# A mixture-of-experts loop on TensorE whose items hold 96 tokens in place of 128

## The reference

```
hn = rms_norm(h, attn_norm[l]);  p = hn @ w_in[l]
h  = h + merged(retention, rwkv7, latent attention) @ w_o[l]
hn = rms_norm(h, ffn_norm[l])
layer 0: h = h + (silu(hn @ wg) * (hn @ wu)) @ wd          # 1024 -> 2816 -> 1024
layer 1: logits = hn @ router; top 2 of 8 experts, softmax over the two
         for e in range(8): out += comb[:, e] * (silu(hn @ wg[e]) * (hn @ wu[e])) @ wd[e]   # 1024 -> 3584 -> 1024
final rms_norm
```

## Time and profile before

| | |
|---|---|
| median of 3 runs | 1890.06 us |
| the profiled execution | 1890.98 us, its span 1888.9 us |
| PE (TensorE matmul) busy | 1853.0 us, 98% |
| PEld (TensorE weight load) busy | 1506.2 us, 80% |
| DVE (VectorE) busy | 1442.5 us, 76% |
| ACT (ScalarE) busy | 1167.1 us, 62% |
| chain that ended last | PE 87%; line L1852 alone 47% |
| mean granted TensorE clock | 0.995 |

### The profile page before, as it was taken

The page is one execution under the profiler, slowest core; times in us unless marked ns, Lnnn a source line. Parts: engine busy times, 40 slices in busy tenths (PEclk is TensorE's granted clock), DMA queues, the critical chain, the costliest instruction groups (busy, mean ns, idle before and its releaser), DMA issues.

```text
span 1888.9 us, 26671 instructions
## 1 busy us (share of the span) xinstructions
PE 1853.0 (98%) x10298; PEld 1506.2 (80%) x10298; DVE 1442.5 (76%) x1487; ACT 1167.1 (62%) x1153; POOL 173.7 (9%) x164
## 2 busy tenths in 40 slices
PE   8999999999999999999999999999999999999998
PEld 7878766788888787767888888888888888888886
DVE  4778575644556785755988989888889899898997
ACT  4575324543444753345777777777777777777776
POOL 1263003100002630040000000000000000000000
PEclk9999999999999999999999999999999999999999
DMA  9642223654566422225999999999999999999995
GB/s 315 207 158 101 90 90 134 217 193 147 188 220 199 158 101 90 90 90 194 358 371 341 368 343 355 366 339 370 342 358 371 352 355 362 342 368 341 360 370 216
DMA packets 182541, 487.79 MB, mean 258 GB/s; under 512 B 5896, under 2 KB 12676, under 8 KB 173640
## 3 DMA queue, kind: packets, MB, share of 16 engines
q1 hardware_dynamic: 177296, 477.50, 69.1%
q0 software_dynamic: 1488, 5.57, 0.9%
q10 hardware_dynamic: 3688, 3.74, 0.7%
HBM read 482.03 MB, written 1.05 MB: 256 GB/s over the span
## 4 chain that ended last, share of the span: by engine, by line
PE 87%; DVE 7%; DMA 3%; ACT 2%; issue 1%; POOL 0%; ACTq 0%; SPq 0%; DVEq 0%
PE bank L1852 47%; PE bank L1249 25%; PE bank L1462 2%; PE bank L1801 2%; PE bank L1433 1%; PE bank L1863 1%; PE bank L1241 1%; DMA ring<-w_o_dram 1%; PE bank L1821 1%; DVE y_rwkv L1920 1%; DVE ring_lo L1920 1%; DMA cst<-const_dram 1%; DVE tmp L1920 1%; DMA ring<-moe_w_down_dram 1%; DMA h<-x_dram 0%
## 5 line engine op out<-in xcount | busy, mean ns | idle before, releaser
L1920 DVE TENSOR_TENSOR w_lo<-ring,w_hi 128x2048 fp32r<-128x2048 f32 x337 | 767.2, 2289 | 112.5 <-ACT w_hi L1151 104.5
L1151 ACT ACTIVATE w_hi<-ring 128x2048 fp32r<-128x2048 f32 x320 | 612.4, 1917 | 122.6 <-PE bank L1852 110.2
L1852 PE MATMUL bank<-w_hi,xg_hi 128*128 128x512 f32 x896 | 354.8, 396 | 1.1 <-DVE w_lo L1920 1.1
L1852 PE MATMUL bank<-w_hi,xg_lo 128*128 128x512 f32 x896 | 349.3, 390 | 0.0
L1852 PE MATMUL bank<-w_lo,xg_hi 128*128 128x512 f32 x896 | 349.0, 389 | 0.0
L1852 PEld LDWEIGHTS bank<-w_hi,xg_hi 128*128 128x128 f32 x896 | 168.8, 188 | 37.5 <-DVE w_lo L1920 4.2
L1852 PEld LDWEIGHTS bank<-w_hi,xg_lo 128*128 128x128 f32 x896 | 168.2, 188 | 35.9
L1852 PEld LDWEIGHTS bank<-w_lo,xg_hi 128*128 128x128 f32 x896 | 168.4, 188 | 33.5 <-issue 0.2
L1852 PE MATMUL bank<-w_hi,ehT_hi 128*128 128x512 f32 x448 | 176.9, 395 | 0.1
L1852 PE MATMUL bank<-w_hi,ehT_lo 128*128 128x512 f32 x448 | 174.7, 390 | 0.0
L1852 PE MATMUL bank<-w_lo,ehT_hi 128*128 128x512 f32 x448 | 174.4, 389 | 0.0
(11 more groups left out here) (434 smaller groups left out, 3027.0 us busy)
## 6 DMA issues: line engine op xcount, KB each, us to landing
ring<-moe_w_gate_dram SPq DMA_DIRECT2D x57, 2048.0 KB, 7.5
ring<-moe_w_up_dram SPq DMA_DIRECT2D x56, 2048.0 KB, 7.7
ring<-moe_w_down_dram SPq DMA_DIRECT2D x56, 2048.0 KB, 9.5
ring<-w_in_dram SPq DMA_DIRECT2D x26, 2048.0 KB, 8.0
ring<-w_branch_dram SPq DMA_DIRECT2D x6, 2048.0 KB, 8.3
ring<-ffn_w_gate_dram SPq DMA_DIRECT2D x5, 2048.0 KB, 7.9
ring<-ffn_w_up_dram SPq DMA_DIRECT2D x5, 2048.0 KB, 7.9
ring<-ffn_w_down_dram SPq DMA_DIRECT2D x5, 2048.0 KB, 8.5
```

The source lines that it names most:

```text
L1151: A.activation(w_hi[:, q % PARTS, :], ring[:, i, o:o + HALF], ACT.Copy).then_inc(s.hi_ready, 1)
L1852: ins = M(dst, a, w, start=start and n == 0, stop=stop and n == 2, skip_group_check=True)
L1920: return V.tensor_tensor(out_, a, b, op)
```

## The change

The constant `CAP = 96` takes the place of `P = 128` wherever it meant "tokens of an item". An item's token columns 0 to 95 are computed; the tiles that rest in the array keep their distance of 128 elements (512 bytes) in SBUF and are read as `[:, x, 0:CAP]`. An expert now needs a second item over 96 tokens and a third over 192: `GROUPS = 3` tables of slots and weights in place of 2, up to `MORE = 5` items beyond the 8 in place of 3, and a longer computation of the list `items`. The moved columns of gate, up, down and scatter stay 512, and the list of matmuls is the same.

```diff
+CAP = 96
+GROUPS = -(-SEQ // CAP)
+MORE = (SEQ * 2 - NE) // CAP
-    c["slots"] = np.tile(np.arange(P, dtype=np.float64), (P, 1))
+    c["slots"] = np.tile(np.where(i < CAP, i, 0.5), (P, 1))
+    c["later"] = np.tile(2 * NE - np.arange(2 * NE, dtype=np.float64), (P, 1))
...
# gather and its two readers
-  ins = M(b[:, i * P:(i + 1) * P], hn[:, t, n * P:n * P + P], sel[:, t, :], start=t == 0,
+  ins = M(b[:, i * CAP:(i + 1) * CAP], hn[:, t, n * P:n * P + P], sel[:, t, 0:CAP], start=t == 0,
-  ins = A.activation(xg_hi[:, 4 * u + i, :], b[:, i * P:(i + 1) * P], ACT.Copy,
+  ins = A.activation(xg_hi[:, 4 * u + i, 0:CAP], b[:, i * CAP:(i + 1) * CAP], ACT.Copy,
-  ins = V.scalar_tensor_tensor(out=xg_lo[:, c, :], in0=b[:, i * P:(i + 1) * P],
+  ins = V.scalar_tensor_tensor(out=xg_lo[:, c, 0:CAP], in0=b[:, i * CAP:(i + 1) * CAP],
...
# gate, up, down
-  ins = three(b[:], xg_hi[:, x, :], xg_lo[:, x, :], q % PARTS,
+  ins = three(b[0:CAP, :], xg_hi[:, x, 0:CAP], xg_lo[:, x, 0:CAP], q % PARTS,
-  ins = three(b[:], ehT_hi[:, x, :], ehT_lo[:, x, :], q % PARTS,
+  ins = three(b[0:CAP, :], ehT_hi[:, x, 0:CAP], ehT_lo[:, x, 0:CAP], q % PARTS,
...
# turn, scatter, transposes of sel
-  ins = TR(b[:, c * P:(c + 1) * P], ehm[:, j % 2, c:512:4], ident)
+  ins = TR(b[:, c * CAP:(c + 1) * CAP], ehm[0:CAP, j % 2, c:512:4], ident[0:CAP, 0:CAP])
-  ins = M(b[:], selT[:, t * P:(t + 1) * P], part[:, 512 * u:512 * u + 512], start=i == 0,
+  ins = M(b[:], selT[0:CAP, t * P:(t + 1) * P], part[0:CAP, 512 * u:512 * u + 512], start=i == 0,
-  ins = TR(b[:, t * P:(t + 1) * P], sel[:, t, :], ident)
+  ins = TR(b[0:CAP, t * P:(t + 1) * P], sel[:, t, 0:CAP], ident)
...
# SiLU, product, and the halves of ehT on ScalarE and VectorE
-  A.activation(esg[:, j % 2, :], item_product(f"eg{j}")[:], ACT.Silu).then_inc(s.freed_act, 1)
+  A.activation(esg[0:CAP, j % 2, :], item_product(f"eg{j}")[0:CAP, :], ACT.Silu).then_inc(s.freed_act, 1)
-  A.activation(ehT_hi[:, 4 * j:4 * j + 4, :],
-               item_product(f"eT{j}")[:].rearrange("p (c n) -> p c n", c=4),
+  A.activation(ehT_hi[:, 4 * j:4 * j + 4, 0:CAP],
+               item_product(f"eT{j}")[:, 0:4 * CAP].rearrange("p (c n) -> p c n", c=4),
-  tt(ehm[:, j % 2, :], b[:], esg[:, j % 2, :], ALU.mult).then_inc(s.freed_vec, 1)
+  tt(ehm[0:CAP, j % 2, :], b[0:CAP, :], esg[0:CAP, j % 2, :], ALU.mult).then_inc(s.freed_vec, 1)
...
# routing: slots per group, flags over 96 and over 192 tokens
-  for i in range(2):
-      step(V.tensor_scalar(spos[:, i, :, :], R(5), -1.0 - P * i, None, ALU.add))
+  for i in range(GROUPS):
+      step(V.tensor_scalar(spos[:, i, :, :], R(5), -1.0 - CAP * i, None, ALU.add))
-  free(V.tensor_scalar(f[:, 0:8], b[0:1, 16:24], P + 0.5, None, ALU.is_gt), "rank.1")
+  step(V.tensor_scalar(f[:, 0:8], b[0:1, 16:24], CAP + 0.5, None, ALU.is_gt))
+  free(V.tensor_scalar(f[:, 8:16], b[0:1, 16:24], 2 * CAP + 0.5, None, ALU.is_gt), "rank.1")
# list of items: 12 small operations with 6 waits between them become 14 with 8 waits
-  step(V.tensor_copy(items[0:1, 0:25], f[:, 32:57]), s.items_ready)
+  step(V.tensor_copy(items[0:1, 0:27], f[:, 56:83]), s.items_ready)
```

More of the change, by code:

```diff
@@ L412, in build @@
     rope_tmp = sb("rope_tmp", [P, 1024], where=B + 49152)
+    pos_f = sb("pos_f", [P, T], where=B + 51200)
     ix_hi = sb("ix_hi", [P, KD, SEQ], F32R, where=ec_at - 4096)
@@ L686, in _ @@
         sp.wait_ge(s.items_ready, 1)
-        n_items = sp.value_load(items[0:1, 24:25], min_val=SURE, max_val=SURE + 3)
+        n_items = sp.value_load(items[0:1, 26:27], min_val=SURE, max_val=SURE + MORE)
         with sp.If(n_items > SURE):
             with sp.Fori(SURE, n_items) as item:
-                e = sp.value_load(items[0:1, bass.ds(item + 12, 1)], min_val=0, max_val=NE - 1)
+                e = sp.value_load(items[0:1, bass.ds(item + NE + MORE, 1)], min_val=0, max_val=NE - 1)
                 expert_panels(e, item)
@@ L1134, in _ @@
         act.wait_ge(s.items_ready, 1)
-        n_items = act.value_load(items[0:1, 24:25], min_val=SURE, max_val=SURE + 3)
+        n_items = act.value_load(items[0:1, 26:27], min_val=SURE, max_val=SURE + MORE)
         with act.Fori(0, n_items) as item:
@@ L1811, in _ @@
         pe.wait_ge(s.items_ready, 1)
-        n_items = pe.value_load(items[0:1, 24:25], min_val=SURE, max_val=SURE + 3)
+        n_items = pe.value_load(items[0:1, 26:27], min_val=SURE, max_val=SURE + MORE)
         def scatter(item, b_of):
@@ L2464, in _ @@
         settle()
-        step(V.tensor_scalar(selT[:], cst[:, 0:SEQ], 0.0, None, ALU.mult))
+        step(V.tensor_scalar(selT[0:CAP, :], cst[0:CAP, 0:SEQ], 0.0, None, ALU.mult))
         step(V.memset(weight[:], 0.0))
         select(0)
-        step(V.tensor_scalar(f[:, 8:16], C("experts")[0:1, :], -1.0, 8.0, ALU.mult, ALU.add))
+        more = slice(0, MORE)
+        over, first, upper = f[:, 24:32][:, more], f[:, 32:40][:, more], f[:, 40:48][:, more]
+        step(tt(f[:, 64:80], C("later")[0:1, :], f[:, 0:16], ALU.mult))
@@ L2470, in _ @@
+        step(V.reduce_sum(f[:, 56 + 26:56 + 27], f[:, 0:16], AX.X))
         settle()
-        step(tt(f[:, 8:16], f[:, 8:16], f[:, 0:8], ALU.mult))
-        step(V.reduce_sum(f[:, 56:57], f[:, 0:8], AX.X))
+        step(V.max(f[:, 16:24], f[:, 64:80]))
         settle()
-        step(V.max(f[:, 16:24], f[:, 8:16]))
+        step(V.tensor_scalar(over, f[:, 16:24][:, more], -1.0, 2.0 * NE, ALU.mult, ALU.add))
+        step(V.tensor_scalar(f[:, 82:83], f[:, 82:83], float(NE), None, ALU.add))
         settle()
-        step(V.tensor_scalar(f[:, 40:44], f[:, 16:20], -1.0, 24.0, ALU.mult, ALU.add))
@@ L2477, in _ @@
-        step(V.tensor_copy(f[:, 32:40], C("experts")[0:1, :]))
-        step(V.tensor_copy(f[:, 44:52], C("experts")[0:1, :]))
-        step(V.tensor_scalar(f[:, 52:56], f[:, 16:20], -1.0, 8.0, ALU.mult, ALU.add))
-        step(V.tensor_scalar(f[:, 56:57], f[:, 56:57], float(NE), None, ALU.add))
+        step(V.tensor_scalar(over, over, 2.0 * NE - 1, None, ALU.min))
         settle()
-        step(V.tensor_scalar(f[:, 52:56], f[:, 52:56], float(NE - 1), None, ALU.min))
-        step(V.tensor_scalar(f[:, 40:44], f[:, 40:44], float(2 * NE * T // 2 + NE - 1), None, ALU.min))
+        step(V.tensor_scalar(upper, over, NE - 0.5, float(NE), ALU.is_gt, ALU.mult))
@@ L2484, in _ @@
         settle()
-        step(V.tensor_copy(items[0:1, 0:25], f[:, 32:57]), s.items_ready)
+        step(tt(first, over, upper, ALU.add))
+        step(tt(over, over, upper, ALU.subtract))
+        settle()
+        step(V.tensor_scalar(f[:, 56 + NE:56 + NE + MORE], first, float(NE * T), None, ALU.add))
+        step(V.tensor_copy(f[:, 56 + 2 * NE + MORE:56 + 2 * NE + 2 * MORE], over))
+        step(V.tensor_copy(f[:, 56:56 + NE], C("experts")[0:1, :]))
+        step(V.tensor_copy(f[:, 56 + NE + MORE:56 + 2 * NE + MORE], C("experts")[0:1, :]))
@@ L2529, in _ @@
         gathered_lo(lambda job: ahead(dve, job), 0)
-        n_items = dve.value_load(items[0:1, 24:25], min_val=SURE, max_val=SURE + 3)
+        n_items = dve.value_load(items[0:1, 26:27], min_val=SURE, max_val=SURE + MORE)
         with dve.Fori(0, n_items) as item:
-            next_column = dve.value_load(items[0:1, bass.ds(item + 1, 1)], min_val=0, max_val=NE * T + NE - 1)
+            next_column = dve.value_load(items[0:1, bass.ds(item + 1, 1)], min_val=0, max_val=NE * T * (GROUPS - 1) + NE - 1)
             def item_product(job):
@@ L2571, in _ @@
                     dve.wait_ge(s.x_hi_ready, item * 9 + (j + 3))
-                    tt(ehT_lo[:, 4 * j:4 * j + 4, :], b[:].rearrange("p (c n) -> p c n", c=4),
-                       ehT_hi[:, 4 * j:4 * j + 4, :].bitcast(F32), ALU.subtract).then_inc(s.freed_vec, 1)
+                    tt(ehT_lo[:, 4 * j:4 * j + 4, 0:CAP], b[:, 0:4 * CAP].rearrange("p (c n) -> p c n", c=4),
+                       ehT_hi[:, 4 * j:4 * j + 4, 0:CAP].bitcast(F32), ALU.subtract).then_inc(s.freed_vec, 1)
                 if q == 35:
```

18 lines of the change are left out of this document (9 added, 9 removed).

## The result

The changed kernel takes 1898.33 us (median of 5 runs, 1896.89 to 1901.92) against 1891.79 for the kernel before (median of 5 runs): a ratio of 1.0040, with an interval of 1.0029 to 1.0051. That is 0.4% slower. One of the five runs of the kernel before took 2428.71 us; it is left out of the ratio, and without it that median is 1890.93. The forecast was 1888.4 with a range up to 1893.5, so both the direction and the range were missed. The profiled execution took 1896.89 us.

What follows compares the result with a forecast made beforehand. TensorE was taken as the bound, with the price of its fp32r matmuls the whole question. All terms were 0 except 1.7 us gained at exposed loads: 1890.06 - 1.7 = 1888.4 us, range 1873 to 1893.5.

Steps and rivals of the forecast that it cites:

- the row at the low clock: At clock 0.50, 512-column matmuls take 0.4275 us against 0.4267 streamed; taken as evidence that fewer resting columns gain zero.
- the matmuls of gate, up and down: Expert loop's 4032 matmuls: resting 96 columns in place of 128 gains zero, at most 13.5 us.
- the 13.4 ns: Time each gate, up or down matmul takes beyond its 0.2133 us stream of 512 columns at full clock.
- Gather: Item start, 32 matmuls: moving columns fall to 96, but the 128-column load sets the pace, gain 0; otherwise 6.8 us.
- Turn: Transposes of `ehm`: the strided 128-column load sets the pace, so 96 moving columns gain 0; otherwise 5 us.
- What follows a gather or a turn: Exposed load and shorter stream before it, eight places per item: 0.027 us less each, 1.7 us gained in all.
- ScalarE and VectorE: Copies into `ehT_hi`, `ehT_lo`, `xg_hi`, `xg_lo` lose a quarter of their columns; that goes into idle time: 0.
- Routing: Extra table, flag, weights and longer list before the loop: hidden, 0; without cover 0.65 us once.
- A: Gate, up and down matmuls speed up with fewer resting columns: 0.2234 us each, 1874.9 us total; chance 0.18.
- B: Gather and turn are bound by the moving stream, so they shorten: 1876.6 us, gather alone 1881.6; chance 0.09.
- D: A ninth item is needed once an expert has 97 tokens: 123.8 us more, 2013.9 us; chance 0.01.
- C: Loads under 128 columns are prepared worse: over 300 us, or mildly 1897.3 us through 64 exposed loads; chance 0.12.

Runs made afterwards that it cites:

- the sweep: Kernel before, with gate and up panel pairs resting on different column counts from 128 down to 32, in two kernels: never under the full tile's 226.9 ns per matmul.
- the resting columns alone: Kernel before with only gate, up and down resting on 96 columns, all else at 128: 1900.11 us against 1890.76, ratio 1.0050.
- the rest of the change alone: Changed kernel with gate, up and down resting on 128 columns again: 1891.98 us against 1890.76, ratio 1.0006.

## Why the prediction was wrong, point by point

**The step that failed** is "I take zero, by the row at the low clock, and keep 13.5 us for the range", for the matmuls of gate, up and down. The term is +2.3 ns on the average, +9.3 us over 4032 matmuls, where the text allowed 0 to -13.5. In the steady middle of a panel it is +3.3 ns (226.7 to 230.0); the average is lower because in the kernel before the six matmuls after each turn already took 228 to 236 ns. The sign that the prediction had named for itself showed it: gather to gather 124.71 us in place of 123.6, more than its 0.5 off. Two things were wrong in it. The rows it used speak of whether a load is exposed as a whole, and are read to 10 ns, while the term is 3; and it bounded an unknown cost from one side only, with the reason that less rests. A bound on the slow side was due, because no row of before had an fp32r matmul on 96 resting columns. That the 13.4 ns are no piece of the load that shrinks with its columns was right, and the sweep shows it: 32 columns cost 231.6. But the row at the low clock didn't say that they are a constant, and they aren't: distance and counts move them between 13 and 20 ns.

**What bounds the kernel** was right: TensorE by its stream of fp32r matmuls, and the price of one is "the whole question".

**Gather.** Right at 0: 32 matmuls in 3.71 us in place of 3.74; (3.71 - 0.25) / 31 is 0.112 each, so the load of 128 columns sets the pace. **Turn.** Right at 0 for the transposes.

**What follows a gather or a turn.** Right. From the last full matmul to the second after the turn it was 0.94 us, now it is 0.91; the loads after a gather went from 0.11 to 0.09 apart.

```profile
1327.41 0.39 PE L1852 MATMUL bank<-w_hi,xg_lo 128*128 128x512 f32 x1
...
1328.35 0.39 PE L1852 MATMUL bank<-w_lo,xg_hi 128*128 128x512 f32 x1
```

It takes both halves of the change, as the text had it: with the resting columns alone that stretch is 0.940 us, with the rest of the change alone 0.938, with both 0.914 (before 0.937). In sum it is 1.5 us, by the item of the resting columns alone against that of the full change: (124.90 - 124.71) x 8. The forecast had 1.7.

**ScalarE and VectorE** at 0: right, they wait more than before. **Routing** at 0: right. Behind the cast of the longer list VectorE still idles before `xg_lo`, 0.29 us where the earlier trace rows had 1.07:

```profile
880.10 0.17 DVE L2496 CAST items<-it_f 1x27 int32<-1x27 f32 x1
...
882.01 0.99 DVE L2520 SCALAR_TENSOR_TENSOR xg_lo<-bank,gains,xg_hi 128x96 fp32r<-128x96 f32 x4 [0.29 <-ACT xg_hi L1127]
```

So 0.78 us of that cover are used, where I had estimated 0.5 to 0.65; some 0.15 us of it is ScalarE, whose copies of 96 columns are ready that much sooner after the gather's start (`xg_lo` starts 3.09 us after it in place of 3.24).

**The rivals.** A (pace follows the resting columns, 1874.9) was wrong in sign. At 512 moving columns no panel of any kernel ran steadily below 226.7. B was wrong, by the gather. D was wrong: x896 again. C had the sign and, in its mild form, nearly the time (1897.3), but its mechanism is refuted: the loads became shorter and the 64 exposed places faster; the loss sits where the load is hidden. That the two numbers agree is chance.

On the fast load that rival C weighed: the Trainium skill (TensorE: Matmul & The Clock Gate, "Weight-path perf modes — Fast Weight Load (FWL) and DoubleRow") says that fewer than 128 resting columns forfeit it. Here the load of 96 columns lasts 0.161 to 0.163 us and that of 128 lasted 0.188; it shrank with the columns, so nothing fast was lost. That would agree with the rule's exclusion of FP32 if fp32r falls under it, which the page doesn't say. The Trainium skill (the same page, "Back-to-back issue gap") gives about 216 ns for an isolated matmul of 512 columns and about 131 ns for one in a sustained stream of loads and matmuls; the fp32r matmuls of such a stream took 226.7 to 233.3 here depending on the placement, above both, and for this kernel the measurement decides.

**What was right in the end.** With the tiles placed at 144 bytes the steady pace is the 226.7 that I forecast, and the kernel takes 1888.17 us, where the forecast said 1888.4. That the two agree to 0.2 us is in part chance: the item is 0.38 us shorter than before (123.44 against 123.82), 3.0 us in eight, where the forecast had 1.7, and the medians differ by 2.5. The forecast described that kernel, not this one. The change as made kept the distance that suits 128 columns.

## What to carry to other kernels

When TensorE is busy all the time, read the distance between starts over nine or more matmuls, not the busy share or the duration of one: both stayed as they were while every matmul became 1.4% dearer. The pace of this stream of fp32r matmuls depended on the distance in the partition between the resting and the moving tile together with both column counts, so a change of any of the three (a narrower item, a tile moved to make room) needs that pace measured anew, over a few distances in steps of 16 bytes. Look at it panel by panel and item by item, because a mean can hide two paces, and prefer a distance at which all panels are fast. And bound an operation that no row shows from both sides, also when it has less to do.

## What the runs showed of the hardware that was not expected

- Moving the resting tiles by 128 bytes, with only addresses changed, costs 1.2% (1912.14 against 1891.01 us); moving resting and moving tiles together costs nothing (1890.55 against 1890.78). For full tiles the effect repeats with 256 bytes (226.9 at 0 and at 256).
- The spacing runs in short patterns, not in noise: 229, 229, 231, 231 ns in the changed kernel, 226 and 227 in the kernel before, 229 and 237 at 128 bytes. All steady values lie between 226.7 and some 233.5 ns for 512 moving columns, 13 to 20 ns over the bare stream of 213.3.
- 32 resting columns (231.6) are dearer than 128 (226.9) at distance 0.
- At some distances the same panel has two steady paces: 226.7 in four items and 233.3 in four with 128 columns at 16 bytes, 233.3 in gate and 226.7 in up panels with 96 columns at 224 bytes.

What stays open: what in the chip couples the two tiles, and what chooses between two paces at one distance. The runs show that distance and both counts matter and that the effect spreads to neighbouring matmuls of another width; that two readers of the same memory get in each other's way would fit, but no run here separates that from other causes, none ran the stream without ScalarE, VectorE and the DMA using the memory beside it, and none says why it is 144 bytes that suit 96 columns. No distance between the steps of 16 bytes was tried, and not `ehT` apart from `xg`.
